# Building the M6 and M7 weight sums with accumulating transfers, and another order of the last products and scalings

## The chip, the cores and the metric

The kernel runs on one core of one Trainium2 chip. The metric is the device time in microseconds; the median of three runs before the change was 672.02 us (671.67 to 672.49). The core has a matrix engine (PE, with its weight loads shown as PEld), a vector engine (DVE), a scalar engine (ACT) and GpSimd (POOL). SyncE (SP) issues most transfers, and 16 DMA engines carry them out.

## The reference, cut to what matters

An encoder block: RMSNorm, one input projection, two attention mixers whose gated outputs are laid side by side, then an output projection, a residual sum and a last RMSNorm. The change lies wholly in the last part:

```python
mixed = jnp.concatenate([out_a, out_b], axis=-1)          # (512, 2048)
x = x + jnp.einsum('bsc,cd->bsd', mixed, w_out)           # 2048 x 2048
return rms_norm(x, final_norm_w)
```

## The kernel before, in words

All matrix products are made in three passes: each operand is split into a high part (rounded to float32r, the PE's format) and a low part (the rest), and high by high, high by low and low by high are summed (`three`, L1396). ACT makes high parts by copying, DVE or POOL makes low parts by subtracting.

The output has 512 tokens, four tiles of 128 rows (`t`), and 2048 columns in four blocks of 512 (`n`). Blocks 0 and 1 are made as plain products over `w_out`. Blocks 2 and 3 are made by Strassen's scheme with seven products M1 to M7 instead of eight: sums of the activations (`u_*`, or the parts of `mixed` as they are) times sums of weight pieces. This stage runs in 16 visits `v`. Each visit reads a buffer `t_raw[v % 4]` of four pieces of 512 columns (1 MB, slots 0 to 3) that SP loads from `w_pairs`. In visits 0 to 7, one sum is made (slots 2:4 become the difference). In visits 8 to 15:

- group 0 of the visit is slots 0:2: slot 0 becomes slot 0 + slot 1 (`part_sums`, L1257), the weights of M1; slot 1 is as loaded, for M5;
- group 1 is slots 2:4: they become slots 2:4 + slots 0:2 (L1255), the weights of M6 and M7.

For each group ACT makes the high part (`part_high`, L732), DVE the low part (`part_low`, L1264), and then PE runs its products: 12 matmuls for group 0 (M5, M1) and 12 for group 1 (M6, M7). DVE's order is fixed: low part of group 0 of visit v, the sums of visit v + 1, low part of group 1 of visit v. `t_hi` has two buffers and `t_raw` four, so ACT waits for PE to be done with the visit two before (`t_used`), and SP loads visit v when PE is done with visit v - 4. When visit 7 is through, DVE adds six finished PSUM banks into `y` (eight adds, `add`, L1277), and PE's products of visit 8 wait for them one after another (`y_added`), since they start in the same banks. In DVE's queue these eight adds stand behind the low part of group 1 of visit 8.

The last two visits, 14 and 15, run product by product: M1, M5, M6, M7 for the tiles 0 and 1 (`q` = 0), then the same for the tiles 2 and 3 (`q` = 1). Each is finished in turn (`m_done` 7 to 14); DVE adds it to `y`, and when a tile's blocks are complete ACT squares them (L705), DVE sums the squares (L1348), ACT takes the root (L790), DVE the reciprocal (L1352). Then each block of the tile is scaled: by ACT (L796), by POOL (L427), by DVE together with the gain `fw` (L1357), or alone (L1363), where POOL had multiplied the gain in ahead of time (`gained`, L402). The tiles come in the order 1, 0, 3, 2. SP stores a tile as two halves: the left one when `left[t]` is 2, the right one when `right[t]` is 2, strictly in this order (L325 to L329).

## Time and profile before

| | us |
|---|---|
| median of three runs | 672.02 |
| the profiled execution's own time | 671.85 |
| its span | 670.1 |
| PE busy | 654.7 (98%) |
| DVE busy | 442.2 (66%) |
| ACT busy | 331.3 (49%) |
| POOL busy | 280.1 (42%) |

The profiled execution is 0.17 us from the median, so its durations can be set against the runs. The span is what the profiler saw from first to last instruction; 1.75 us of the execution lie around it. PE is busy nearly all the time, so it sets the pace; the shares of the others are averages over stages, and say little of the last 60 us, where the change lies. A time there is given in us from the start of the span.

### The profile page before, as it was taken

To read this page: it belongs to the slowest core of one execution; us is meant where nothing else is said; L and a number is where in the kernel's file an instruction comes from. 1 tells how busy PE (TensorE), PEld (TensorE's weight loads), DVE (VectorE), ACT (ScalarE), POOL (GpSimd) and SP (SyncE) were. 2 spreads that over 40 slices of the span, in tenths; PEclk is the share of its full clock that TensorE was granted. 3 is DMA by queue.
4 is the path that set the end of the run, shared out by engine and by line. 5 is a ranking of instruction groups with operands and counts; after the bars stand their busy time and mean duration, and the time that the engine had idled before them with its cause. 6 is when DMAs were issued, how large, how long until landed. Compare 5 with 4: busy or idle time off the path is not lost. (4 is left out here: it accounts for less than half of the span.)

```text
span 670.1 us, 8800 instructions
## 1 busy us (share of the span) xinstructions
PE 654.7 (98%) x3126; PEld 548.4 (82%) x3126; DVE 442.2 (66%) x702; ACT 331.3 (49%) x623; POOL 280.1 (42%) x135
## 2 busy tenths in 40 slices
PE   9999999999999999999999999999999999999893
PEld 8888888888888888888888888888888888787782
DVE  6788132889684554654645667777553769899985
ACT  6743231311343753763664566877864533543534
POOL 0044443454244433433532526747868483020204
PEclk9999999999999999999999999999999999999997
DMA  8742322232232222222212413213124813576416
GB/s 293 256 141 96 103 94 95 83 105 95 94 94 96 75 83 95 92 65 95 95 64 94 126 35 124 64 64 96 32 72 177 299 65 113 233 259 236 180 64 251
DMA packets 21656, 81.96 MB, mean 122 GB/s; under 512 B 2416, under 2 KB 2672, under 8 KB 19568
## 3 DMA queue, kind: packets, MB, share of 16 engines
q1 hardware_dynamic: 18000, 73.41, 32.1%
q10 hardware_dynamic: 3616, 8.02, 3.4%
q8 instruction: 25, 0.41, 0.2%
q14 instruction: 15, 0.12, 0.1%
HBM read 77.22 MB, written 4.19 MB: 122 GB/s over the span
## 5 line engine op out<-in xcount | busy, mean ns | idle before, releaser
L337 POOL TENSOR_TENSOR w_lo<-w_raw,w_hi 128x1024 fp32r<-128x1024 f32 x84 | 206.0, 2458 | 269.7 <-ACT w_hi L442 269.6
L1398 PE MATMUL bank<-x_hi,w_hi 128*128 128x512 f32 x496 | 193.7, 390 | 0.0
L1401 PE MATMUL bank<-x_hi,w_lo 128*128 128x512 f32 x496 | 193.3, 390 | 0.0
L1402 PE MATMUL bank<-x_lo,w_hi 128*128 128x512 f32 x496 | 193.2, 390 | 0.0
L442 ACT ACTIVATE w_hi<-w_raw 128x1024 fp32r<-128x1024 f32 x93 | 98.1, 1055 | 130.0 <-PE bank L1398 109.1
L1402 PEld LDWEIGHTS bank<-x_lo,w_hi 128*128 128x128 f32 x496 | 93.1, 188 | 19.7
L1398 PEld LDWEIGHTS bank<-x_hi,w_hi 128*128 128x128 f32 x496 | 93.2, 188 | 18.8 <-DVE mixed L1078 0.5
L1401 PEld LDWEIGHTS bank<-x_hi,w_lo 128*128 128x128 f32 x496 | 93.2, 188 | 18.0
L402 POOL TENSOR_TENSOR y<-y,fw 128x512 f32<-128x512 f32 x11 | 17.6, 1616 | 80.1 <-ACT junk L705 44.4
L1398 PE MATMUL bank<-w_hi,mx_hi 128*128 128x512 f32 x128 | 50.3, 393 | 0.0
L1402 PE MATMUL bank<-w_lo,mx_hi 128*128 128x512 f32 x128 | 49.9, 390 | 0.0
L1401 PE MATMUL bank<-w_hi,mx_lo 128*128 128x512 f32 x128 | 49.9, 390 | 0.0
L732 ACT ACTIVATE t_hi<-t_raw 128x1024 fp32r<-128x1024 f32 (+1 forms) x32 | 29.8, 950 | 37.7 <-DVE t_raw L1257 19.5
L540 ACT ACTIVATE bank<-pa,st_a 128x128 f32<-128x128 f32 x64 | 22.8, 356 | 43.2 <-DVE st_a L992 43.2
L1264 DVE TENSOR_TENSOR t_lo<-t_raw,t_hi 128x1024 fp32r<-128x1024 f32 (+1 forms) x32 | 35.2, 1120 | 5.3 <-ACT t_hi L732 5.3
L1007 DVE TENSOR_TENSOR pta_lo<-bank,pta_hi 128x512 fp32r<-128x512 f32 x16 | 11.1, 692 | 32.1 <-ACT pta_hi L547 32.0
L1402 PEld LDWEIGHTS bank<-w_lo,mx_hi 128*128 128x128 f32 x128 | 24.0, 188 | 5.1
L1401 PEld LDWEIGHTS bank<-w_hi,mx_lo 128*128 128x128 f32 x128 | 24.1, 188 | 4.7
L895 DVE TENSOR_TENSOR t<-bank,sin_r 32x512 f32<-32x512 f32 x40 | 27.5, 687 | 0.5
L1398 PEld LDWEIGHTS bank<-w_hi,mx_hi 128*128 128x128 f32 x128 | 24.0, 188 | 4.6
L1015 DVE TENSOR_TENSOR mixed<-bank,o_low 64x256 f32<-64x256 f32 x32 | 13.5, 422 | 21.6 <-ACT o_low L554 21.4
L1398 PE MATMUL bank<-t_hi,mx_hi 128*128 128x512 f32 x64 | 25.3, 395 | 2.3 <-DVE t_lo L1264 2.2
(242 smaller groups left out, 1236.0 us busy)
## 6 DMA issues: line engine op xcount, KB each, us to landing
w_raw<-w_stream SPq DMA_DIRECT2D x93, 512.0 KB, 3.3
t_raw<-w_pairs SPq DMA_DIRECT2D x15, 1024.0 KB, 4.7
y<-x_nat ACTq DMA_DIRECT2D x4, 1024.0 KB, 5.3
out<-y SPq DMA_DIRECT2D x8, 512.0 KB, 3.0
xs<-x_t SPq DMA_DIRECT2D x4, 512.0 KB, 5.5
mixed<-x_t SPq DMA_DIRECT2D x4, 512.0 KB, 5.6
t_raw<-w_pairs ACTq DMA_DIRECT2D x1, 1024.0 KB, 7.7
fw<-final_w ACTq DMA_DIRECT2D x4, 256.0 KB, 5.6
```

The costliest lines, as they stand in the source:

```text
L337: pool.tensor_tensor(w_lo[:, s % HL, :], w_raw[:, s % RAW, :], w_hi[:, s % HL, :].bitcast(F32), ALU.subtract)\
L402: pool.tensor_tensor(y[:, t, cols], y[:, t, cols], fw[n][:, :], ALU.mult).then_inc(o_gained, 1)
L442: act.activation(w_hi[:, s % HL, :], w_raw[:, s % RAW, :], ACT.Copy).then_inc(w_hi_ready, 1)
L540: act.activation(B[4][:, P * k:P * k + P], pa[:, slot, k, :], ACT.Exp, bias=st[:, 1, k:k + 1], scale=A_SCALE, accum_out=st[:, 3, k:k + 1])
L732: act.activation(t_hi[v % 2][:, s, :], t_raw[v % 4][:, s, :], ACT.Copy).then_inc(t_high, 1)
L895: ins = dve.tensor_tensor(t2[32 * q:32 * q + 32, :], src[32 * o:32 * o + 32, :], sin[32 * q:32 * q + 32, :], ALU.mult)
L1007: dve.tensor_tensor(pta_lo[:, :], B[6][:, :], pta_hi[:, :].bitcast(F32), ALU.subtract).then_inc(a_pt_lo, 1)
L1015: ins = dve.tensor_tensor(out_e, by_head[h, e], o_low[h, :, :, :], ALU.add)
L1264: dve.tensor_tensor(t_lo[v % 4][:, s, :], t_raw[v % 4][:, s, :], t_hi[v % 2][:, s, :].bitcast(F32), ALU.subtract).then_inc(t_low[g], 1)
L1398: ins = pe.matmul(dst, ah, bh, start=start, stop=False, skip_group_check=goes_on)
L1401: pe.matmul(dst, al, bh, start=False, stop=False, skip_group_check=goes_on)
L1402: return pe.matmul(dst, ah, bl, start=False, stop=stop, skip_group_check=goes_on)
```

## The change

Three things are changed.

1. In visits 8 to 15 the group 1 sum is made by a transfer. When the load of visit v has landed, POOL issues a transfer that reads slots 0:2 from `w_pairs` in device memory once more (0.5 MB) and adds them to slots 2:4 in place. DVE's L1255 is gone; ACT's `part_high(v, 1)` waits for the new semaphore `t_added` instead. On POOL, the two gain products of block 2 now wait for DVE's low parts of visits 11 and 12.
2. In the last products for tiles 2 and 3, M6 comes ahead of M5. DVE's adds, ACT's squares and the row sums are put in an order that goes with it.
3. POOL scales with `tensor_tensor` and a broadcast operand instead of `tensor_scalar`, and takes over ACT's scaling of block 0 of tile 3.

```diff
+            def piece_added(v):
+                pool.wait_ge(t_landed[v % 4], 16 * (v // 4) + 16)
+                pool.dma_start(t_raw[v % 4][:, 2:4, :], w_pairs[v, :, 0:2, :], accum_op=ALU.add).then_inc(t_added[v % 4], 16)
+
             pool.wait_ge(fw1_landed, 16)
             for t in range(TOK):
                 pool.wait_ge(o_squared, 4 + t + 2)
                 pool.wait_ge(t_low[1], 4 + t)
                 gained(t, 1)
+                if t == 2:
+                    piece_added(8)
+            piece_added(9)
+            piece_added(10)
+            piece_added(11)
+            piece_added(12)
             pool.wait_ge(fws_landed, 32)
             for q in range(2):
                 pool.wait_ge(o_squared, 8 + q + 2)
+                pool.wait_ge(t_low[1], 12 + q)
                 gained(2 * q + 1, 2)
+                piece_added(13 + q)
+            piece_added(15)
...
-                pool.tensor_scalar(ys, ys, fin[:, t, 2:3], None, ALU.mult).then_inc(side[t], 1)
+                pool.tensor_tensor(ys, ys, fin[:, t, 2:3].to_broadcast([P, SEQ]), ALU.mult).then_inc(side[t], 1)
...
+            scale(2, 3, 0, 8, left)
             scale(2, 3, 1, 8, left)
...
                 if g == 0 and v < 8:
                     act.wait_ge(t_landed[v % 4], 16 * (v // 4) + 16)
+                elif g == 1 and v >= 8:
+                    act.wait_ge(t_added[v % 4], 16 * (v // 4) - 16)
                 else:
-                    act.wait_ge(t_summed, v + 1 if v < 8 else 2 * v - 6 - (g == 1))
+                    act.wait_ge(t_summed, v + 1)
...
             last_square(1, 3, 11, 13)
+            root(0, 1)
             last_square(0, 2, 12, 14)
-            root(0, 1)
+            root(1, 0)
             scale(0, 1, 2)
-            root(1, 0)
-            last_square(2, 3, 13, 17)
             scale(1, 0, 1)
-            last_square(3, 3, 14, 19)
+            last_square(3, 3, 13, 17)
+            last_square(2, 3, 14, 18)
+            root(2, 3)
             last_square(2, 2, 15, 20)
-            root(2, 3)
             root(3, 2)
-            scale(2, 3, 1)
             scale(3, 2, 2)
...
-                    dve.tensor_tensor(raw[:, 2:4, :], raw[:, 2:4, :], raw[:, 0:2, :], ALU.add).then_inc(t_summed, 1)
-                    dve.wait_ge(t_summed, 2 * v - 7)
                     dve.tensor_tensor(raw[:, 0, :], raw[:, 0, :], raw[:, 1, :], ALU.add).then_inc(t_summed, 1)
...
+            row_sum(0, 1, 13)
             add(0, 2, 0, 10, 12, op=ALU.subtract)
-            row_sum(0, 1, 13)
-            row_sum(1, 0, 14)
             reciprocal(0, 1)
             scale_gain(0, 1, 3)
+            row_sum(1, 0, 14)
             add(2, 2, 5, 11)
+            reciprocal(1, 0)
             add(3, 3, 5, 11, 4)
-            reciprocal(1, 0)
...
             m1(15, 1).then_inc(m_done, 1)
+            m6(14, 1)
+            m6(15, 1).then_inc(m_done, 1)
             m5(14, 1)
             m5(15, 1).then_inc(m_done, 1)
-            m6(14, 1)
-            m6(15, 1).then_inc(m_done, 1)
```

The rest of DVE's order at the end is shown below in its instructions. `add(3, 3, 7, ...)` stands for block 3 of tile 3 from bank 7.

POOL's queue from the gain products of block 1 to its end (`t_raw_60` to `t_raw_63` are the buffers 0 to 3), as the difference of the two:

```order
-L402 TENSOR_TENSOR y<-y,fw_169 128x512 [waits t_low1,o_squared] x3
-L402 TENSOR_TENSOR y<-y,fw_170 128x512 [waits o_squared,fws_landed]
-L402 TENSOR_TENSOR y<-y,fw_170 128x512 [waits o_squared]
+L402 TENSOR_TENSOR y<-y,fw_169 128x512 [waits t_low1,o_squared] x2
+L413 DMA t_raw_60<-w_pairs 128x1024 [waits t_landed0]
+L402 TENSOR_TENSOR y<-y,fw_169 128x512 [waits t_low1,o_squared]
+L413 DMA t_raw_61<-w_pairs 128x1024 [waits t_landed1]
+L413 DMA t_raw_62<-w_pairs 128x1024 [waits t_landed2]
```

The accumulating transfer of visit 8 stands ahead of the last gain product of block 1, those of 9 and 10 (and of 11 and 12) behind it.

DVE's queue around visit 8, before:

```order
L1255 TENSOR_TENSOR t_raw0_60<-t_raw0_60 128x1024 [waits t_landed0]
L1257 TENSOR_TENSOR t_raw0_60<-t_raw0_60 128x512 [waits t_summed]
L1264 TENSOR_TENSOR t_lo3_67<-t_raw3_63,t_hi1_69 128x1024 [waits t_high]
L1264 TENSOR_TENSOR t_lo0_64<-t_raw0_60,t_hi0_68 128x1024 [waits t_high]
L1255 TENSOR_TENSOR t_raw1_61<-t_raw1_61 128x1024 [waits t_landed1]
L1257 TENSOR_TENSOR t_raw1_61<-t_raw1_61 128x512 [waits t_summed]
L1264 TENSOR_TENSOR t_lo0_64<-t_raw0_60,t_hi0_68 128x1024 [waits t_high]
L1277 TENSOR_TENSOR y_147<-y_147,bank4 128x512 [waits m_done,y_landed]
```

and now:

```order
L1270 TENSOR_TENSOR t_raw0_60<-t_raw0_60 128x512 [waits t_landed0]
L1277 TENSOR_TENSOR t_lo3_67<-t_raw3_63,t_hi1_69 128x1024 [waits t_high]
L1277 TENSOR_TENSOR t_lo0_64<-t_raw0_60,t_hi0_68 128x1024 [waits t_high]
L1270 TENSOR_TENSOR t_raw1_61<-t_raw1_61 128x512 [waits t_landed1]
L1277 TENSOR_TENSOR t_lo0_64<-t_raw0_60,t_hi0_68 128x1024 [waits t_high]
L1290 TENSOR_TENSOR y_147<-y_147,bank4 128x512 [waits m_done,y_landed]
```

The two large sums are gone; the first of the eight adds still stands behind the low part of group 1 of visit 8 (the fifth row), whose high part now waits for the new transfer.

DVE's queue at the end of the tiles 3 and 2, from the first add of M1's bank 5, before:

```order
L1277 TENSOR_TENSOR y_147<-y_147,bank5 128x512 [waits m_done]
L1277 TENSOR_TENSOR y_147<-y_147,bank5 128x512 [waits y_added,m_done]
L1352 RECIPROCAL fin_83<-fin_83 128x1 [waits o_root]
L1277 TENSOR_TENSOR y_147<-y_147,bank3 128x512 [waits y_added,m_done] x2
L1277 TENSOR_TENSOR y_147<-y_147,bank7 128x512 [waits y_added,m_done]
L1357 SCALAR_TENSOR_TENSOR y_147<-y_147,fin_83,fw2_170 128x512 [waits o_recip]
L1277 TENSOR_TENSOR y_147<-y_147,bank1 128x512 [waits y_added,m_done]
L1348 TENSOR_REDUCE fin_83<-sumsq_82 128x1 [waits o_squared]
```

and now:

```order
L1290 TENSOR_TENSOR y_147<-y_147,bank5 128x512 [waits m_done]
L1365 RECIPROCAL fin_83<-fin_83 128x1 [waits o_root]
L1290 TENSOR_TENSOR y_147<-y_147,bank5 128x512 [waits y_added,m_done]
L1290 TENSOR_TENSOR y_147<-y_147,bank7 128x512 [waits y_added,m_done]
L1370 SCALAR_TENSOR_TENSOR y_147<-y_147,fin_83,fw2_170 128x512 [waits o_recip]
L1290 TENSOR_TENSOR y_147<-y_147,bank3 128x512 [waits y_added,m_done] x2
L1361 TENSOR_REDUCE fin_83<-sumsq_82 128x1 [waits o_squared]
L1290 TENSOR_TENSOR y_147<-y_147,bank1 128x512 [waits y_added,m_done]
```

The add of M6's bank 7, which completes tile 3, moves ahead of the two adds of M5's bank 3, and tile 3's sum of squares ahead of the last add.

## Rows read from the trace of the kernel before

**Rows 1.** The page: the whole span.
```profile
PE 654.7 (98%) x3126; PEld 548.4 (82%) x3126; DVE 442.2 (66%) x702; ACT 331.3 (49%) x623; POOL 280.1 (42%) x135
```
**Rows 2.** Busy time of each engine by stretch; then clock, DMA share, GB/s.
```profile
612.00:618.00 6.00, 5.65 (x23) 3.86 (x22) 6.00 (x10) 0.63 (x1) 0.00 (x0) 1.00 0.71 265
618.00:630.00 12.00, 10.05 (x44) 7.99 (x43) 10.80 (x9) 6.83 (x10) 3.53 (x2) 1.00 0.47 175
630.00:648.00 18.00, 18.00 (x81) 14.88 (x81) 15.91 (x16) 7.80 (x8) 0.00 (x0) 1.00 0.35 117
```
**Rows 3.** Timeline of PE's weight loads and matmuls: start, duration, instruction, idle before.
```profile
612.96 0.19 PEld L1398 LDWEIGHTS bank<-t_hi,u_hi 128*128 128x128 f32 x1 [0.55 <-DVE y L1277]
614.16 0.19 PEld L1398 LDWEIGHTS bank<-t_hi,u_hi 128*128 128x128 f32 x1 [0.66 <-DVE y L1277]
617.68 0.19 PEld L1398 LDWEIGHTS bank<-t_hi,u_hi 128*128 128x128 f32 x1 [0.26 <-DVE t_lo L1264]
628.09 0.19 PEld L1398 LDWEIGHTS bank<-t_hi,mx_hi 128*128 128x128 f32 x1 [2.37 <-DVE t_lo L1264]
...
657.74 0.39 PE L1401 MATMUL bank<-t_hi,mx_lo 128*128 128x512 f32 x1
657.97 0.39 PE L1402 MATMUL bank<-t_lo,mx_hi 128*128 128x512 f32 x1
```
**Rows 4.** Timeline of DVE, visits 8 to 12.
```profile
604.00 1.64 DVE L1255 TENSOR_TENSOR t_raw<-t_raw 128x1024 f32<-128x1024 f32 x1 [0.59 <-DMA t_raw<-w_pairs]
...
610.50 1.22 DVE L1264 TENSOR_TENSOR t_lo<-t_raw,t_hi 128x1024 fp32r<-128x1024 f32 x1
611.63 4.87 DVE L1277 TENSOR_TENSOR y<-y,bank 128x512 f32<-128x512 f32 x8
616.41 2.36 DVE L1264 TENSOR_TENSOR t_lo<-t_raw,t_hi 128x1024 fp32r<-128x1024 f32 x2
...
624.15 1.67 DVE L1257 TENSOR_TENSOR t_raw<-t_raw 128x512 f32<-128x512 f32 x1
625.74 3.43 DVE L1264 TENSOR_TENSOR t_lo<-t_raw,t_hi 128x1024 fp32r<-128x1024 f32 x2
...
630.34 0.69 DVE L1257 TENSOR_TENSOR t_raw<-t_raw 128x512 f32<-128x512 f32 x1
630.95 2.44 DVE L1264 TENSOR_TENSOR t_lo<-t_raw,t_hi 128x1024 fp32r<-128x1024 f32 x2
```
**Rows 5.** Groups by line from 540 us on: busy, mean ns, idle before.
```profile
L732 ACT ACTIVATE t_hi<-t_raw 128x1024 fp32r<-128x1024 f32 x24 | 25.0, 1058 | 33.8 <-DVE t_raw L1257 19.5 <-PE bank L1402 13.9 <-DVE t_raw L1253 0.4
L1255 DVE TENSOR_TENSOR t_raw<-t_raw 128x1024 f32<-128x1024 f32 x8 | 10.2, 1270 | 0.6 <-DMA t_raw<-w_pairs 0.6
```
**Rows 6.** DMA issues of the whole span: KB each, median us to landing.
```profile
t_raw<-w_pairs SPq DMA_DIRECT2D x15, 1024.0 KB, 4.7
out<-y SPq DMA_DIRECT2D x8, 512.0 KB, 3.0
t_raw<-w_pairs ACTq DMA_DIRECT2D x1, 1024.0 KB, 7.7
```
**Rows 7.** SP's queue, and bandwidth from 600 to 612 us in 40 slices.
```profile
603.34 0.33 SPq L324 DMA_DIRECT2D t_raw<-w_pairs  x1
GB/s 191 27 55 164 437 410 437 410 437 437 437 55 0 0 109 0 218 273 410 410 437 437 437 437 328 0 0 0 164 82 273 273 382 437 437 437 437 410 164 0
```
**Rows 8.** Timeline of the end: POOL, DVE, ACT and SP's queue.
```profile
652.47 1.30 POOL L402 TENSOR_TENSOR y<-y,fw 128x512 f32<-128x512 f32 x1 [25.52 <-ACT junk L705]
660.86 0.16 DVE L1352 RECIPROCAL fin<-fin 128x1 f32<-128x1 f32 x1 [0.91 <-ACT fin L790]
661.12 2.12 POOL L427 TENSOR_SCALAR y<-y,fin 128x512 f32<-128x512 f32 x1 [0.48 <-DVE fin L1352]
663.27 0.33 SPq L327 DMA_DIRECT2D out<-y  x1
```
**Rows 9.** Timeline of POOL: two gain products beside DVE's work.
```profile
623.42 3.53 POOL L402 TENSOR_TENSOR y<-y,fw 128x512 f32<-128x512 f32 x2 [18.87 <-ACT junk L705]
```

More of the change, by code:

```diff
@@ L266, in build @@
         fw1_landed = sem("fw1_landed")
-        t_landed = [sem(f"t_landed{n}") for n in range(4)]
+        t_landed, t_added = ([sem(f"{name}{n}") for n in range(4)] for name in ("t_landed", "t_added"))
         u_summed, u_high, u_low, p_summed, p_high, p_low = sem("u_summed"), sem("u_high"), sem("u_low"), sem("p_summed"), sem("p_high"), sem("p_low")
@@ L1370, in _ @@
             add(1, 3, 6, 9, 10)
+            row_sum(0, 1, 13)
             add(0, 2, 0, 10, 12, op=ALU.subtract)
-            row_sum(0, 1, 13)
-            row_sum(1, 0, 14)
             reciprocal(0, 1)
             scale_gain(0, 1, 3)
+            row_sum(1, 0, 14)
             add(2, 2, 5, 11)
+            reciprocal(1, 0)
             add(3, 3, 5, 11, 4)
-            reciprocal(1, 0)
-            add(2, 3, 3, 12, 6)
-            add(2, 2, 3, 12, 15, op=ALU.subtract)
-            add(3, 3, 7, 13, 16)
+            add(3, 3, 7, 12, 16)
             scale_gain(1, 0, 2)
-            add(2, 2, 1, 14, 18, op=ALU.subtract)
-            row_sum(2, 3, 16)
+            add(2, 3, 3, 13, 6)
+            add(2, 2, 3, 13, 15, op=ALU.subtract)
+            row_sum(2, 3, 15)
+            add(2, 2, 1, 14, 19, op=ALU.subtract)
             reciprocal(2, 3)
             scale_gain(2, 3, 3)
+            scale(2, 3, 2, 10)
             row_sum(3, 2, 17)
-            scale(2, 3, 2, 10)
             reciprocal(3, 2)
```

## The prediction

> **What bounds the kernel now.** I read the page first: PE is busy for 98% of the span [rows 1], so time is won only where PE stands still or where the end hangs behind its last product. The busy times by stretch then say where it stands still: in 630 to 648 not at all, in 612 to 618 for 0.35 us, in 618 to 630 for 1.95 us [rows 2]. The timeline of the weight loads names the places [rows 3]. A load runs one matmul ahead, so about 0.26 us of its idle time are made up: the idle of 0.55, 0.66, 0.26 and 2.37 us costs PE about 0.29, 0.40, 0 and 2.11 us, 2.80 in all. The first two wait for the eight adds behind visit 7, the long one for a low part of visit 10: all three for DVE. DVE's timeline shows why [rows 4]: from 604.0 on it works without a gap. Visit 8's large sum, the low part at 610.50 and then the eight adds, which start at 611.63, follow each other; the next low parts can't start ahead of 616.41; and around 624 to 629 its steps are stretched, the small sum to 1.67 us and two low parts to 3.43, where later visits show 0.69 and 2.44 [rows 4]. POOL runs two gain products there, 3.53 us [rows 9]. So of 2.80 us that can be won in this stretch, 2.11 depend on how much DVE has to do in visits 9 to 11, and 0.69 on when the eight adds start. The rest of the time until the last matmul at 657.97 [rows 3] PE paces itself.
>
> **Part 1, the sums by transfer: what goes.** Eight large sums of DVE, 10.2 us busy, 1.27 us each [rows 5], one in each visit. A visit has 24 matmuls at 0.23 us (the last two of [rows 3]), 5.4 us, and DVE then has two low parts (2.44) and a small sum (0.6 to 0.7) [rows 4] in it, 3.1 us. It has slack from there on. Does the 2.11 us stall at 628.09 go? Take the adds to start at 611.85 (below). They end at 616.65; two low parts of visit 9 take 2.3 (616.41 to 618.68 before), to 618.95; the small sum 0.6, to 619.6; ACT's copy 1.06 [rows 5], to 620.7; the low part 1.15, to 621.9; the next small sum, to 622.5; the low part that PE waited for, to 623.7. PE will want it after visits 8 and 9 and half of visit 10, at about 626. So 2.3 us are to spare and the stall goes: -2.11. The gain products that stretched DVE now wait for the low parts of visits 11 and 12 and fall later, at about 630 and 636; if they stretch DVE there by the 2.0 us seen before (1.67 - 0.69 and 3.43 - 2.44 [rows 4]), the 2.3 us of slack that each visit has covers it.
>
> **Part 1: what comes.** The high part of group 1 waits for load, then transfer, then ACT, then DVE. What is queued behind it matters: on DVE, behind the low part of group 1 of visit 8, stand the eight adds for which PE waits at once. Call L the time from visit 8's landing (604.0, when DVE's wait for it ends [rows 4]) to the landing of the accumulating transfer. POOL is free to issue it at once, since the gain product that held it is put behind it. Then the adds start at 604.0 + L + 1.06 (ACT's copy [rows 5]) + 1.13 (from 610.50 to 611.63 [rows 4]) + some 0.06 of semaphores = 606.25 + L. Before they started at 611.63, and PE lost 0.69 us. So visit 8 changes by (606.25 + L) - 611.63 = L - 5.4 us, and not below -0.69, which is reached at L = 4.7. With the -2.11 the whole stage changes by L - 7.5 us, at best by -2.8.
>
> No row shows an accumulating transfer, or one that POOL issues. From below, a plain store of as many bytes lands after 3.0 us; from above, the slowest load of twice the bytes after 7.7 us and two usual ones after each other after 9.4 (4.7 each) [rows 6]. Between the ends I build it from a load. Visit 9's load is issued at 603.34, its data flow from about 604.8 to 607.6 at up to 437 GB/s, the first 1.5 us after the issue [rows 7]. The new transfer's first data would come 1.5 us after 604.0, at 605.5, with 2.1 us of visit 9's data still to come on the same DMA engines. If only its 0.5 MB count (1.2 us at that rate), and the engines are shared evenly, it needs 2.4 us; if the read of its destination counts like another 0.5 MB, 2.4 us of its own and 2.1 of the other's, 4.5. With 0.6 us from last data to landing, as for visit 8's load (603.3 to about 604.0), L is 4.5 or 6.6. I take the middle, 5.6: the adds at 611.85, PE's stall in visit 8 0.9 instead of 0.7, the stage -1.9 us.
>
> The Trainium skill (DMA: Bandwidth & Descriptors, "Anatomy of one DMA — SWDGE (gpsimd) path") gives for a transfer issued by GpSimd some 2.0 us and its bytes over 436 GB/s, an estimate of 3.2 us for these 0.5 MB; it says nothing of accumulation, and no run here shows it yet. By that rule L would be under 4.7 and the stage -2.8.
>
> For visits 9 to 15 L costs nothing up to about 12 us: the load goes out when PE ends visit v - 4, and group 1 is wanted three and a half visits later, 19 us, of which 4.7 go to the load and 2.3 to ACT and DVE. 4 MB more cross the DMA engines in these 45 us, which were used to 0.71, 0.47 and 0.35 [rows 2]; SP's loads may land up to 1 us later, which the same 19 us cover. POOL's queue waits for nothing there that is late: visit 13's transfer stands behind a gain product that runs at about 630, when its load has just landed.
>
> **Parts 2 and 3, the end.** PE's number of matmuls is the same. With M6 ahead of M5, tile 3 is complete 1.36 us (six matmuls) earlier, and tile 2's block 3 as much later, where it isn't last: M7's product is. What ends the run is the stores. Of the last four, the first is issued at 663.27 when tile 3's left half is ready; and the end, 670.1, comes 6.8 us later: 2.1 MB at 437 GB/s are 4.8 us, and 1.5 from issue to first data and 0.6 behind the last [rows 7] make 6.9, so the last four stores run in a row. So the end moves with that first store, not with the last scaling. Before, tile 3's reciprocal came at 660.86 because ACT squared tile 2's last block ahead of its root; POOL then scaled one block in 2.12 us, to 663.24 [rows 8]. Now the root comes ahead of that square, and by ACT's and DVE's orders the reciprocal comes about 0.8 us earlier. But POOL does two blocks in a row. The new form, two operands, took 1.30 us for a gain product when DVE read one operand from its own memory [rows 8], and 1.77 when DVE's work had two (3.53 for two [rows 9]). Two blocks: 2.6, 3.5, or, if broadcasting costs what `tensor_scalar` did, 4.2 us. From about 660.2 that is 662.8, 663.7 or 664.4, against 663.24: -0.4, +0.5, +1.2. I take 1.6 each, nearest to the mixture beside it: +0.1.
>
> The Trainium skill (SBUF — State Buffer, "Who interferes with whom") says that a DVE instruction with two inputs in SBUF contends with GpSimd's reads. The trace agrees (1.30 against 1.77). DVE's scalings there have two such inputs, so by the rule alone the end would be +0.5; by the row without such a neighbour -0.4.
>
> **The sum.** -2.1 (stall in visit 10), +0.2 (visit 8), +0.1 (end) = -1.8 us. The profiled execution's own 671.85 becomes 670.05; from the median, 0.17 higher, 670.2.
>
> **The rivals.**
> - The transfer is short, L below 4.7. For it: the store's 3.0 us, and the row for 1 MB, 4.7. Against: it reads its destination too, and shares the engines. Stage -2.8, end +0.1: 669.3.
> - The saving is paid back in visit 8: L near 7.7, the slowest load of the trace. For it: every add waits behind this one transfer, and it comes just when visit 9's load has the engines full [rows 7]. Stage +0.2, end +0.1: 672.3.
> - Slower: an accumulating transfer is slow in itself. It decides from L = 8.8 on (8.8 - 7.5 = 1.3, the bound of what is told from no change). At L = 10, 2.5 us more: 674.6. For it: reading, adding and writing back may not be overlapped in the DMA engines as a copy is; two loads after each other are 9.4. Its place would be visit 8 alone, PE waiting for the adds for some 5 us.
> - That the transfers do the sums but DVE's relief is worth nothing, because the 2.11 us wait turns into one for ACT or POOL: the chain above has 2.3 us to spare, so little speaks for it. 671.9 or so.
>
> **How the numbers follow.** A measurement of this kernel tells about 0.2%, 1.34 us, from no change. The forecast holds 0.33, the short transfer 0.22, pay-back 0.25, slower 0.17, the last 0.03. The forecast's own range is L from 4.7 to 6.2, with the end's -0.4 to +0.5: 669.0 to 671.0. Faster, L below about 6.1: 0.55. Slower 0.18. Within: 0.27. The range: at the low end -2.8 and -0.4, 668.8; at the high end L = 9.4, +1.9, with the end's +0.1: 674.0.
>
> **What would show it.** In the new profile: the time from visit 8's landing to the start of ACT's copy of group 1 is L; DVE's eight adds start 2.2 us later; PE's only stall of note stands in visit 8, and none at visit 10; DVE has idle time in each of visits 10 to 15. At the end the store of tile 3's left half is issued 5.4 us after PE's last matmul starts, where it was 5.3. I would be wrong if L is above 6.2, if POOL issues the first transfer late, or if a wait for `t_added` shows up on PE's side in a visit other than 8.

## The result, and the profile after

The changed kernel takes **678.95 us** (median of 4 runs, 678.17 to 681.86); the kernel before, run beside it, 672.25 (671.67 to 673.46). The ratio is 1.0107, 95% interval 1.009 to 1.0124: slower by 6.7 us, where 670.2 was forecast, and outside the range (668.8 to 674.0). The profiled execution took 678.73 us by its own time, with a span of 676.9, against 671.85 and 670.1 before; both kernels are compared by these.

The page of the changed kernel answers to [rows 1] and [rows 6]:

```profile
PE 656.8 (97%) x3126; PEld 550.0 (81%) x3126; DVE 436.0 (64%) x694; ACT 330.7 (49%) x622; POOL 287.6 (42%) x144
...
t_raw<-w_pairs SPq DMA_DIRECT2D x15, 1024.0 KB, 5.7
...
t_raw<-w_pairs POOLq DMA_DIRECT2D x8, 512.0 KB, 7.6
out<-y SPq DMA_DIRECT2D x8, 512.0 KB, 3.5
```

DVE has eight instructions less, as forecast. The eight accumulating transfers take 7.6 us to land in the median for half a megabyte, longer than a load of a whole one took before (4.7), and the loads have become slower beside them.

The last matmul starts at 663.97, 6.0 us later than before [rows 3]; the span ends 12.9 us behind it, where it was 12.1. So 6.0 us arose while PE still multiplied and 0.8 at the end. The weight loads that waited longest name the places (start, duration, instruction, idle before it and what ended it):

```profile
615.66 0.19 PEld L1411 LDWEIGHTS bank<-t_hi,u_hi 128*128 128x128 f32 x1 [3.12 <-DVE y L1290]
616.86 0.21 PEld L1411 LDWEIGHTS bank<-t_hi,u_hi 128*128 128x128 f32 x1 [0.67 <-DVE y L1290]
...
647.12 0.19 PEld L1411 LDWEIGHTS bank<-t_hi,mx_hi 128*128 128x128 f32 x1 [0.91 <-DVE t_lo L1277]
...
652.87 0.19 PEld L1411 LDWEIGHTS bank<-t_hi,u_hi 128*128 128x128 f32 x1 [2.48 <-DVE t_lo L1277]
...
655.86 0.19 PEld L1411 LDWEIGHTS bank<-t_hi,mx_hi 128*128 128x128 f32 x1 [1.07 <-DVE t_lo L1277]
```

Less the 0.26 us that the load's lead makes up, these are 2.86 and 0.41 in visit 8, 0.65 in visit 13, and 2.22 and 0.81 for visit 15's two low parts: 6.95 us, against 2.80 before. The stall of visit 10 is gone. That leaves 1.8 of the 6.0 us, and they are in the clock. Busy time by short stretches behind visit 8's stall (PE, PEld, DVE, ACT, POOL, then granted clock, DMA share, GB/s):

```profile
616.00:618.00 2.00, 1.77 (x6) 1.15 (x5) 2.00 (x5) 0.00 (x0) 0.64 (x1) 0.74 1.03 344
618.00:620.00 2.00, 2.00 (x6) 1.54 (x6) 2.00 (x3) 1.06 (x1) 0.18 (x1) 0.50 1.04 256
620.00:622.00 2.00, 2.00 (x10) 1.61 (x9) 2.00 (x3) 0.00 (x0) 0.68 (x1) 0.90 1.03 218
622.00:624.00 2.00, 2.00 (x10) 1.68 (x9) 0.88 (x2) 1.90 (x2) 0.00 (x0) 1.00 1.00 276
```

From 616.9 to 620.4 the granted clock is 0.5, the lower level of 1.2 GHz (1.00 is 2.4 GHz); weight loads start 0.43 us apart instead of 0.23. Eight matmuls at 0.2 us more each: 1.7 us. So the 3.1 us of idle time (2.86 us of PE's) cost some 4.6. Before, no stretch of 612 to 648 was below 1.00 [rows 2], a stall of 2.37 us in it.

Visit 8's chain, which the prediction followed, in the timeline of POOL, ACT and DVE (it answers to [rows 4]; the transfer's issue is the row on POOL):

```profile
604.49 1.01 POOL L413 DMA_DIRECT2D t_raw<-w_pairs  x1 [3.64 <-DMA t_raw<-w_pairs]
```
```profile
612.10 2.00 ACT L748 ACTIVATE t_hi<-t_raw 128x1024 fp32r<-128x1024 f32 x2 [6.11 <-DMA t_raw<-w_pairs]
```
```profile
604.20 0.69 DVE L1270 TENSOR_TENSOR t_raw<-t_raw 128x512 f32<-128x512 f32 x1 [0.53 <-DMA t_raw<-w_pairs]
...
613.19 1.22 DVE L1277 TENSOR_TENSOR t_lo<-t_raw,t_hi 128x1024 fp32r<-128x1024 f32 x1 [3.46 <-ACT t_hi L748]
614.33 4.86 DVE L1290 TENSOR_TENSOR y<-y,bank 128x512 f32<-128x512 f32 x8
```

Visit 8 lands at 604.2 and its transfer at 612.1: L is 7.9 us, 5.6 was taken. The adds start 2.2 us behind it, as worked out, and PE loses 2.6 us more than before, where "L - 5.4" gives 2.5. The chain was right and L was not.

How full the DMA engines are, by the same stretches as [rows 2] and by queue from 600 to 660 us (packets, MB, share of all 16 engines):

```profile
612.00:618.00 6.00, 3.07 (x11) 1.91 (x10) 4.81 (x8) 2.00 (x2) 0.86 (x1) 0.91 1.04 333
618.00:630.00 12.00, 12.00 (x49) 9.79 (x49) 8.25 (x9) 7.30 (x11) 0.86 (x1) 0.90 0.99 268
630.00:648.00 18.00, 17.51 (x78) 14.20 (x77) 10.71 (x9) 5.77 (x6) 7.69 (x6) 1.00 0.95 250
```
```profile
q1 hardware_dynamic: 1152, 8.39, 38.5%
q0 software_dynamic: 1152, 4.19, 38.5%
...
t_raw<-w_pairs SPq DMA_DIRECT2D x7, 1024.0 KB, 7.9
t_raw<-w_pairs POOLq DMA_DIRECT2D x8, 512.0 KB, 7.6
```

Shares of 0.71, 0.47 and 0.35 [rows 2] became 1.04, 0.99 and 0.95, at a bandwidth far from the 437 GB/s seen in [rows 7]. The transfers' queue (q0) holds the engines as long as the loads' (q1) for half the bytes: 38.5% of 60 us over eight is 2.9 us of all 16 engines for each transfer. With 2.9 for each load that is 5.8 us of DMA for a visit of 5.4 us of matmuls.

The end, DVE's and POOL's timelines (they answer to [rows 8]):

```profile
667.39 0.15 DVE L1365 RECIPROCAL fin<-fin 128x1 f32<-128x1 f32 x1
```
```profile
667.63 2.48 POOL L440 TENSOR_TENSOR y<-y,fin 128x512 f32<-128x512 f32 x2 [2.69 <-DVE fin L1365]
```
```profile
670.14 0.33 SPq L327 DMA_DIRECT2D out<-y  x1
```

Tile 3's left half is stored 6.2 us after the last matmul (5.3 before, 5.4 forecast). POOL is not to blame: its two blocks take 1.24 us each, less than the 1.6 taken. The reciprocal comes 3.4 us after the last matmul, 2.9 before, where 0.8 less was forecast.

### The profile page after: what moved, and what is told of

The parts are those of the page before. It is cut to its first block, busy times and chain, and to the rows that moved or that the text cites. A ratio compares the mean times of both kernels' runs of the same rounds, so it can differ in the third digit from the quotient of the medians.

```text
span 676.9 us, 8799 instructions
## 1 busy us (share of the span) xinstructions
PE 656.8 (97%) x3126; PEld 550.0 (81%) x3126; DVE 436.0 (64%) x694; ACT 330.7 (49%) x622; POOL 287.6 (42%) x144
## 3 DMA queue, kind: packets, MB, share of 16 engines
q0 software_dynamic: 1152, 4.19, 3.4%
HBM read 81.42 MB, written 4.19 MB: 126 GB/s over the span
## 4 chain that ended last, share of the span: by engine, by line
PE 84%; DVE 7%; DMA 4%; issue 3%; ACT 2%; POOL 0%; DVEq 0%; ACTq 0%; POOLq 0%
PE bank L1411 25%; PE bank L1414 25%; PE bank L1415 25%; DMA t_raw<-w_pairs 4%; PE bank L1676 1%; DVE y L1290 1%; PE bank L1555 1%; PE bank L1565 1%; DVE p_sum L1257 1%; DVE t_raw L1268 1%; DVE t_lo L1277 1%; DVE u_lo L1246 1%; PE bank L1441 1%; PE bank L1662 1%; PE bank L1663 1%
## 5 line engine op out<-in xcount | busy, mean ns | idle before, releaser
L402 POOL TENSOR_TENSOR y<-y,fw 128x512 f32<-128x512 f32 x11 | 20.9, 1913 | 47.0 <-DVE t_lo L1277 35.7
```

Of the source, the lines that this page charges most:

```text
L402: pool.tensor_tensor(y[:, t, cols], y[:, t, cols], fw[n][:, :], ALU.mult).then_inc(o_gained, 1)
```

## The experiments

The expectations name their theories by letters. A: the addition makes a transfer take about twice the time of the DMA engines, so load and transfer fill them and pace the stage. B: the way through POOL makes a transfer late, whatever the load on the engines. C: visit 8's transfer is what costs. D: POOL's broadcast form slows DVE at the end. E: the stall of visit 10 came from POOL's gain products. F: the last visits have too little time between load and use.

**Part 1 and parts 2 and 3, apart.** `e1_part1` has the transfers and POOL's two waits with the end as before; `e2_parts23` the new end with DVE's large sums and neither transfers nor waits.

> Part 1 alone: the M6 and M7 sums by accumulating transfers and POOL's waits, with the end as before. The trace of the change shows the last matmul 6.0 us later (663.97 against 657.97) and 0.8 us more behind it (12.9 against 12.1). If that 0.8 belongs to parts 2 and 3, this kernel takes about 678.1 us (5.9 over before), the last matmul again near 664.0. If parts 2 and 3 interact with part 1, for example because DVE reaches the end in another state, it would differ from that by a microsecond or more either way.

> Parts 2 and 3 alone: DVE makes the sums as before, POOL's gain products don't wait for the low parts of visits 11 and 12; the order of the last products and the sharing of scalings as in the change. My prediction's step says the end moves by +0.1 (-0.4 to +1.2): 672.3 us. The trace of the change says +0.8 behind the last matmul: 673.0. With the last matmul at about 658.0 in either case; if it is later, the order of M6 and M5 costs PE something by itself.

Part 1 alone: 677.64 us (676.0 to 678.29), ratio 1.0061 (1.0037 to 1.0086). Its last matmul starts at 663.96, and its end is 12.5 us long: in this trace all of the loss before the end is its own (the profiled execution took 678.29 us, the longest of the four). Parts 2 and 3 alone: 673.26 (672.77 to 674.25), ratio 1.001 (0.9999 to 1.002), the end 13.05 us behind the last matmul at 658.55, 0.9 longer than before. What stretches it is on DVE. `e2_parts23`, timeline of DVE; before, each of these scalings took 0.75 us:

```profile
655.09 1.63 DVE L1380 SCALAR_TENSOR_TENSOR y<-y,fin,fw 128x512 f32<-128x512 f32 x1
...
658.75 1.38 DVE L1380 SCALAR_TENSOR_TENSOR y<-y,fin,fw 128x512 f32<-128x512 f32 x1
```

**POOL's form at the end.** `e5_scalar_pool` is `e2_parts23` with POOL's old instruction:

```
-pool.tensor_tensor(ys, ys, fin[:, t, 2:3].to_broadcast([P, SEQ]), ALU.mult)
+pool.tensor_scalar(ys, ys, fin[:, t, 2:3], None, ALU.mult)
```

> Parts 2 and 3 as in the run of parts 2 and 3 alone, but POOL scales with tensor_scalar as before, not with tensor_tensor and a broadcast operand. In that run DVE's two scalings with gain ahead of tile 3's row sum took 1.63 and 1.37 us where they took 0.75 before, beside POOL's new instructions. Theory D, the broadcast form takes DVE's second operand away: now DVE's two scalings take 0.75 again, tile 3's reciprocal comes 1.5 us earlier, POOL's two blocks take 4.2 instead of 2.5 us, and the store of tile 3's left half is issued at most 0.3 us sooner: 672.9 to 673.4 us, the loss merely moved. Rival, it is the new order of adds, squares and sums that is late: DVE's scalings stay long, or the reciprocal stays late, and the time goes up to 674.5 since POOL is slower.

672.78 us (672.1 to 673.89), ratio 1.0001 (0.999 to 1.0013). DVE's and POOL's timelines:

```profile
655.98 0.75 DVE L1380 SCALAR_TENSOR_TENSOR y<-y,fin,fw 128x512 f32<-128x512 f32 x1
...
658.78 0.74 DVE L1380 SCALAR_TENSOR_TENSOR y<-y,fin,fw 128x512 f32<-128x512 f32 x1
...
661.43 0.16 DVE L1375 RECIPROCAL fin<-fin 128x1 f32<-128x1 f32 x1
```
```profile
661.68 3.66 POOL L447 TENSOR_SCALAR y<-y,fin 128x512 f32<-128x512 f32 x2 [0.44 <-DVE fin L1375]
```

The last matmul starts at 659.45, so the reciprocal comes 1.98 us behind it: 0.9 earlier than before, which is the forecast's 0.8, and 1.5 earlier than in `e2_parts23`, as theory D had it. It is the broadcast form on POOL that stretches these scalings and took this away. But POOL then needs 3.66 us for its two blocks, and the store goes out 5.9 us behind the last matmul. Each form gives back what the new order wins. The two medians lie 0.5 us apart, with overlapping intervals.

The old form isn't free for DVE either. In `e1_part1` and seven more of the traces below that keep the old end (`e7` to `e11`, `e13`, `e14`) the second of DVE's scalings took 1.23 or 1.24 us beside `tensor_scalar` instead of 0.75, POOL's three blocks took 5.21 us instead of 5.75, and the end was 12.5 us long instead of 12.1:

```profile
664.53 1.24 DVE L1370 SCALAR_TENSOR_TENSOR y<-y,fin,fw 128x512 f32<-128x512 f32 x1
```

In `e6_pool_waits` and `e12_last_plain` it was 0.75 and 0.74 us, as before. No run shows what tips it one way or the other.

The trace of `e5_scalar_pool` (673.89 us, the longest of its ten executions) holds something else. It has the stall of visit 10 as the kernel before had it, 2.35 us against 2.37, but here the lower clock followed; weight loads, then busy times:

```profile
627.96 0.19 PEld L1421 LDWEIGHTS bank<-t_hi,mx_hi 128*128 128x128 f32 x1 [2.35 <-DVE t_lo L1287]
```
```profile
630.00:634.00 4.00, 4.00 (x14) 3.23 (x13) 3.97 (x5) 2.12 (x2) 0.00 (x0) 0.71 0.14 16
```

From 629 to 632 the granted clock was 0.50, and the last matmul of this execution came 1.5 us later than before.

**The addition left out.** `e3_plain_copy` is the changed kernel with `accum_op=ALU.add` struck from the transfer, so that M6's and M7's sums are not formed; the same bytes are written at the same place.

> The change with POOL's eight transfers as plain copies instead of accumulating ones: the same bytes from the same place over slots 2:4, so that the addition is left out. Theory A, accumulation is what costs: in the trace of the change a software transfer of 0.5 MB takes as much time on the 16 DMA engines as a load of 1 MB, so load and transfer together take 5.8 us of a visit's 5.4, and the engines pace the stage. A plain copy of 0.5 MB should take half of that, land in about 4.5 to 5.5 us, leave visit 8 a stall under 1 us and none later: 669.5 to 671 us. Rival B, it is the way through POOL (its issue, its descriptors) and not the addition: the time to landing stays at 7 us or more, visit 8's stall of 3 us and the slow clock behind it stay, 676 us or more.

671.72 us (670.91 to 677.45, 11 runs), ratio 0.9989 (0.9978 to 1.0): of 7.2 us between the two kernels all are due to the addition, by the medians. This is theory A's forecast (669.5 to 671) missed by 0.7 us, and far from B's (676 or more).

The profiled execution was the unusual one of 677.45 us. In its trace visit 8's load landed at 606.8, 2.6 us later than in the change, and PE had waited for low parts three times by then (0.37, 0.30 and 0.44 us, from 596 to 605), as it doesn't in the traces of the change and of `e15_plain_copy_again`. Its plain copy had L = 7.6 us, PE stood still for 3.72 us and the lower clock followed until about 624. So a plain copy can be as late as the accumulating one, here in one execution of eleven that was disturbed before. `e15_plain_copy_again` took the same kernel once more.

> The kernel with plain copies (the addition left out) once more, for a profile of a usual execution: the profiled one of the first run took 677.5 us against a median of 671.7. Expected 671.7, the copies landing after 4.5 to 6 us, visit 8's stall under 1.5 us with no slow clock, no stall over 0.6 us in visits 13 to 15.

671.38 us. ACT's timeline, and queues from 600 to 660 us:

```profile
610.00 2.01 ACT L748 ACTIVATE t_hi<-t_raw 128x1024 fp32r<-128x1024 f32 x2 [4.16 <-DMA t_raw<-w_pairs]
```
```profile
q1 hardware_dynamic: 1493, 9.65, 46.1%
q0 software_dynamic: 1152, 4.19, 20.5%
```

With a plain copy L is 5.8 us in this execution, almost the 5.6 that the forecast took, the copies land after 5.7 us in the median instead of 7.6, the same 4.19 MB hold the engines for 20.5% instead of 38.5%, and the clock is at 1.00 in every stretch. The last matmul starts at 656.67, 1.3 us before the old one. So this run is nearly what was forecast: 1.3 us won before the end (1.9 forecast; waits of 1.22 and 0.66 us stand in visit 8, and a new one of 0.49 near the end) and 0.8 lost at the end. The loads still take 7.3 us in the median, against 7.9 in the change and 4.8 before: late loads alone don't make PE wait.

**Adds ahead of the late low part.** `e4_adds_first` is the changed kernel with `part_low(8, 1)` behind the eight adds, which take PE's first two waits off the transfer.

> The change with one move in DVE's order: the eight adds of visit 8 ahead of the low part of its group 1, so that they no longer wait for the first transfer. Theory C, visit 8 is what costs: its 3.3 us stall behind the adds and the 1.7 us of matmuls at half clock behind it shrink to a stall of some 1.7 us for M6, and the kernel gains about 3.3 us, to 675.7. Theory A, the DMA engines pace the stage: what is gained in visit 8 is given back in visits 13 to 15, where PE waits for transfers by so much more, and the time stays within 1.3 us of the change's 679.

677.02 us (675.99 to 679.31), ratio 1.0072 (1.0044 to 1.01); 1.9 us less than the change by the medians, which the intervals don't separate (1.009 to 1.0124), and between the forecasts of C (3.3 less) and A (at most 1.3). The weight loads' waits in its trace (675.99 us, the shortest of four), and busy times behind the last of them:

```profile
615.23 0.19 PEld L1413 LDWEIGHTS bank<-t_hi,mx_hi 128*128 128x128 f32 x1 [1.71 <-DVE t_lo L1277]
629.48 0.19 PEld L1413 LDWEIGHTS bank<-t_hi,u_hi 128*128 128x128 f32 x1 [0.73 <-DVE t_lo L1277]
633.17 0.19 PEld L1413 LDWEIGHTS bank<-t_hi,mx_hi 128*128 128x128 f32 x1 [1.09 <-DVE t_lo L1277]
650.04 0.29 PEld L1413 LDWEIGHTS bank<-t_hi,u_hi 128*128 128x128 f32 x1 [2.68 <-DVE t_lo L1277]
```
```profile
650.00:652.00 2.00, 1.96 (x5) 1.59 (x6) 1.21 (x2) 0.76 (x1) 0.00 (x0) 0.50 0.00 0
```

Visit 8's stall shrinks from 3.3 to 1.45 us and the lower clock behind it goes, but 1.3 us of new stalls in visit 11 take part of that back, and now the lower clock follows visit 15's stall of 2.68 us, where it had stayed at 1.00 behind the change's 2.48. What was won in visit 8 is in large part paid later.

**POOL's waits alone.** `e6_pool_waits` is the kernel before with one line of the change:

```
                 pool.wait_ge(o_squared, 8 + q + 2)
+                pool.wait_ge(t_low[1], 12 + q)
                 gained(2 * q + 1, 2)
```

> The kernel before with one edit of the change alone: POOL's two gain products of block 2 wait for DVE's low parts of visits 11 and 12. Theory E, most of PE's 2.1 us stall in visit 10 comes from these products running beside DVE's sums (its steps are stretched by 2.0 us there): the stall at 628 shrinks to 0.1 to 0.3 us and the kernel takes 670.3 us. Rival, the products stretch DVE later instead and PE stalls as long in visit 12 or 13: 672.0 to 672.3.

670.92 us (670.62 to 672.25), ratio 0.9982 (0.9972 to 0.9992). PE's wait in visit 10 falls from 2.37 to 0.30 us, and a new one comes for visit 15:

```profile
626.05 0.19 PEld L1399 LDWEIGHTS bank<-t_hi,mx_hi 128*128 128x128 f32 x1 [0.30 <-DVE t_lo L1265]
646.95 0.19 PEld L1399 LDWEIGHTS bank<-t_hi,u_hi 128*128 128x128 f32 x1 [1.30 <-DVE t_lo L1265]
```
```profile
631.01 2.20 POOL L402 TENSOR_TENSOR y<-y,fw 128x512 f32<-128x512 f32 x1 [26.44 <-DVE t_lo L1265]
636.29 2.22 POOL L402 TENSOR_TENSOR y<-y,fw 128x512 f32<-128x512 f32 x1 [3.09 <-DVE t_lo L1265]
```

Theory E's stall of 0.1 to 0.3 us came true; its 670.3 us was missed by 0.6, for the new wait. About 1.4 us, most of the gain of 1.8 that was forecast for the whole change, comes from moving two gain products out of DVE's way, with no transfer at all.

**Transfers in some visits only.** All of these have part 1's form with DVE's large sum back in the other visits, and the end as before. `e7_two_visits` has transfers in visits 10 and 11 and no waits on POOL; the others have POOL's waits: visits 9 to 15, then 9, 11, 13, 15, then 9 alone, 9 to 13, and 9, 11, 13.

> The kernel before with accumulating transfers in visits 10 and 11 alone, without POOL's waits and with the end as before. Theory A (the DMA engines pace the stage when load and transfer come in every visit): with two transfers they have room, the stall of visit 8 stays 0.7, DVE saves 2.8 us ahead of the low part that PE waits for in visit 10, the 2.1 us stall goes, no stall comes in visits 13 to 15: 670.3 us. Rival B (a transfer through POOL is late whatever the load on the engines): it lands 7 to 8 us after the load also here.

> Part 1 for visits 9 to 15 only; visit 8's sum stays on DVE, the end as before. Theory C, visit 8's transfer is what costs (2.9 us of stall and 1.7 of half clock): 673 us or less, and no stall of note behind visit 8. Theory A, the engines pace the stage (5.8 us of load and transfer in a visit of 5.4): PE still waits 3 to 4 us in visits 12 to 15: 674 to 676 us.

> Part 1 for visits 9, 11, 13 and 15 only, with POOL's waits and the end as before. Theory A: load and transfer cost about 2.9 us each on all 16 DMA engines, so two visits now need 8.7 us of 10.9; the engines no longer pace the stage. Visit 9's sum goes from DVE's queue ahead of the eight adds, so these start 1.2 us earlier and visit 8's 0.7 us go; POOL's waits take the 2.1 us of visit 10; no stall in visits 13 to 15: 669.5 us. Rival B, the transfers are late whatever the load on the engines: they land 8 us or more after the load, and visits 13 and 15 still make PE wait: 671 us or more.

> The kernel before with one accumulating transfer, visit 9's, and POOL's waits. It is the version that the runs so far point to: the 0.7 us of visit 8 go since the adds start 1.2 us earlier, and the 2.1 us of visit 10 since POOL's gain products are out of the way (1.5 us were measured for the waits alone, which left a stall of 1.3 us in visit 14). 669.8 to 670.3 us. Rival: the transfer lands too late for visit 9's group 1 (wanted 10 us after its load), and a new stall stands there: 671 or more.

> Part 1 for visits 9 to 13 only, POOL's waits, the end as before. Visits 14 and 15 are multiplied product by product: PE wants visit 15's second group 2 visits and 12 matmuls (13.6 us) after visit 11's end, when its load is issued, not 19 us; with 4.7 us of load and 2.3 us of ACT and DVE that leaves 6.6 us for the transfer, which took 7 us and more in the change. Theory F, the short lead at the end is what costs behind visit 8: without transfers in 14 and 15 no stall over 0.5 us stands behind 640, and the time is 670.3 to 671. Theory A, crowded DMA engines (5.8 us of load and transfer in a visit of 5.4): the stalls of visits 10 to 13 (1.2, 0.4 and 0.3 us with transfers from visit 9 on) stay and PE waits 2 us more ahead of 647: 672.5 or more.

> Transfers in visits 9, 11 and 13 only, POOL's waits, the end as before: the run with every other visit, less visit 15. Theory F: its stall of 4.1 us in front of M6 of visits 14 and 15 goes, with the slow clock behind it; what is left is at most the 0.9 us in front of visit 10 that visit 9's late transfer costs, and DVE is relieved where its work is tight: 669.5 to 670.3 us, at or under the best so far (670.6). Rival: with a transfer in visit 13, DVE's low part of visit 14 is late all the same: over 671.

| transfers in visits | POOL's waits | median us (from, to) | ratio, 95% | last matmul |
|---|---|---|---|---|
| none | no | 672.3 | 1 | 657.97 |
| none (`e6`) | yes | 670.92 (670.62, 672.25) | 0.9982 (0.9972, 0.9992) | 657.08 |
| 9 (`e10`) | yes | 670.61 (670.03, 671.61) | 0.9973 (0.996, 0.9985) | 657.31 |
| 10, 11 (`e7`) | no | 670.95 (669.79, 671.95) | 0.9977 (0.9967, 0.9987) | 655.75 |
| 9, 11, 13 (`e14`) | yes | 670.63 (670.05, 674.19) | 0.9985 (0.9971, 0.9999) | 655.75 |
| 9 to 13 (`e13`) | yes | 672.33 (671.98, 673.17) | 1.0005 (0.9995, 1.0015) | 657.64 |
| 9, 11, 13, 15 (`e9`) | yes | 673.38 (671.17, 676.13) | 1.0014 (0.9996, 1.0032) | 660.39 |
| 9 to 15 (`e8`) | yes | 674.16 (672.47, 675.6) | 1.0028 (1.0015, 1.004) | 658.57 |
| 8 to 15 (`e1`) | yes | 677.64 (676.0, 678.29) | 1.0061 (1.0037, 1.0086) | 663.96 |

The last column is of the profiled execution, which lay up to 1.3 us from its median either way (`e8` 673.01 us, `e9` 674.68, `e10` 671.61).

By the medians, visit 8's transfer costs 3.5 us (677.64 - 674.16), those of 14 and 15 1.8 (674.16 - 672.33), and those of 9 to 13 1.4 (672.33 - 670.92), while every other one of these costs nothing (670.63). The differences are good to about 1 us, that of visit 8 to about 2, and 0.4 to 0.5 of the 1.4 is the longer end told above. That end also hides something: in `e7` and `e14` PE is through 1.3 us sooner than in `e6`, and the end is 0.5 longer.

Against the expectations: `e8` (674.16) is at the lower edge of A's 674 to 676, above C's 673. `e13` (672.33) lies nearer to A's 672.5 than to F's 671. `e9` (673.38) missed A's 669.5 by 3.9 and is on B's side, for visit 15's wait below. `e7` (670.95) missed its 670.3 by 0.6; `e10` and `e14` lie between forecast and rival. And B was right on one thing that A had otherwise: with few transfers they still landed late, after 9.7 us in the median in `e7` (two of them) and 7.9 in `e10` (one), each beside loads. Yet PE's waits behind them were short: 0.37 us in `e7`, 0.94 and 0.38 in `e10`.

Two traces show what the number of transfers does to PE's idle time. First `e13_visits_9_to_13`, then `e14_9_11_13`, from 618 us on:

```profile
618.00:630.00 12.00, 11.13 (x49) 8.56 (x48) 5.22 (x6) 6.56 (x10) 1.72 (x2) 1.00 1.03 313
```
```profile
618.00:630.00 12.00, 11.93 (x53) 9.54 (x52) 8.93 (x10) 8.05 (x12) 0.86 (x1) 1.00 0.87 259
```

At a DMA share of 1.03 PE is 0.87 us idle, at 0.87 it is 0.07. (In the change itself PE isn't idle in this stretch at 0.99; it is 4.6 us behind by then, so it wants everything later.) And `e9_every_other` shows that a visit's place counts beside its neighbours: visit 15's transfer, issued at 641.1, had the engines to 0.63 in 630 to 648 and still took 7.4 us. ACT's and PE's timelines:

```profile
648.52 1.06 ACT L755 ACTIVATE t_hi<-t_raw 128x1024 fp32r<-128x1024 f32 x1 [4.97 <-DMA t_raw<-w_pairs]
```
```profile
650.88 0.29 PEld L1422 LDWEIGHTS bank<-t_hi,mx_hi 128*128 128x128 f32 x1 [4.10 <-DVE t_lo L1288]
```

Its last 2 us moved at only 10 to 20 GB/s, which looks like a few DMA engines finishing late (no run here singled them out); and the clock was 0.86 in 648 to 660, the lower level again behind a long wait.

**The transfer by itself.** Visit 15's load is the last, so that nothing else is in flight while its transfer runs. `e11_last_alone` has the transfer in visit 15 only, `e12_last_plain` the same with the addition left out (M6's and M7's last sums are not formed). Each is one execution; the first took 672.3 us, the second 674.86. That second time isn't used: some 1.4 us arose before 615, ahead of any transfer, and the rest behind visit 10's stall, 2.35 us again, where the granted clock was 0.50 from 631 to 634.

> The kernel before with the accumulating transfer in visit 15 alone, whose load is the last one: nothing else is in flight. It measures the transfer by itself. Theory A (crowded DMA engines make it late): it lands after 4.5 to 5 us, against 6.1 to 9.8 in the change. Rival B (accumulating is slow by itself): after 7 us or more. The time stays within 1 us of before in either case.

> The same with a plain copy of the same bytes in place of the accumulating transfer (the addition in visit 15 is left out). If adding costs a second pass over the data on the DMA engines, the copy lands about 1.2 us (0.5 MB at 437 GB/s) earlier than the accumulating one, and its packets take half the time. If the way through POOL is the cost, both land alike.

The queues from 636 to 652 us, with the addition and then without:

```profile
q0 software_dynamic: 144, 0.52, 21.2%
q1 hardware_dynamic: 144, 1.05, 18.5%
...
t_raw<-w_pairs POOLq DMA_DIRECT2D x1, 512.0 KB, 5.6
```
```profile
q0 software_dynamic: 144, 0.52, 10.0%
...
t_raw<-w_pairs POOLq DMA_DIRECT2D x1, 512.0 KB, 4.4
```

Alone, the accumulating transfer takes 5.6 us to land and holds all 16 engines for 3.4 us (21.2% of 16), the plain copy 4.4 and 1.6: 2.1 times the engine time for the same bytes, and 1.2 us on the landing, as the expectation had it. The 5.6 us lie between A's forecast (4.5 to 5) and B's (7 or more). A load of twice the bytes holds them for 3.0 (18.5%).

## Why the prediction was wrong, step by step

Between the 670.2 us forecast and 678.95 lie 8.7 us: 2.3 for L, 3.7 for waits in visits 13 and 15 that had been put at nothing, 1.8 for the clock, 0.7 for the end and 0.2 for the median before, 672.25 instead of 672.02.

- **The 2.11 us stall of visit 10 goes: right in the time, not in the cause.** It is gone in the changed kernel, but in `e6_pool_waits` most of it goes without a transfer. The prediction knew that the gain products would be put later and counted that as harmless instead of as the remedy. `e7_two_visits` shows that relieving DVE by two sums does it as well; the two remedies do not add up.
- **"I take the middle, 5.6": the step that failed first.** L was 7.9 us, and visit 8 costs 2.5 us by the prediction's own formula with that number, where 0.2 was taken. The bounds were built for a transfer whose destination counts as as many bytes again. Alone, a transfer takes 5.6 us from issue to landing (`e11_last_alone`); beside visit 9's load and visit 9's own transfer, issued at 609.3, L is 7.9. The Trainium skill (DMA: Bandwidth & Descriptors, "Anatomy of one DMA — SWDGE (gpsimd) path") has 2.0 us and bytes over 436 GB/s, an estimate of 3.2; the trace disagrees, with 4.4 us for a plain copy alone and 5.6 for an accumulating one, and the text there speaks of no addition.
- **What no step had: the clock.** A stall of 3.1 us was followed by 3.5 us at the lower level, 1.7 us more (1.8 is what the sum of the waits leaves). The prediction's slower case priced its stall by its length alone: at L = 7.9 this adds more than half of what the stall itself adds.
- **"For visits 9 to 15 L costs nothing up to about 12 us": false, twice, and the dearest step, 3.7 us.** "Used to 0.71, 0.47 and 0.35" with 4 MB more were counted by bytes; by engine time each accumulated byte counts double, and 5.8 us of DMA per visit do not fit into 5.4, so the lead is used up. The loads went from 4.8 to 7.9 us in these 60 us; but with plain copies they took 7.3, so it is the transfers, 7.6 instead of 5.7, that the addition made late. That the doubled engine time is what makes them so is argued from the shares, and `e7` shows 9.7 us at a mean share of 0.88 (612 to 630). And 19 us of lead are not to be had at the end of the row, where visits 14 and 15 are multiplied product by product. Visit 15's group 1 is wanted (PE's queue waits for it ahead of M6 of visit 14) two visits and 12 matmuls after its load goes out, 13.6 us; load 7.9, transfer 7.3 and ACT and DVE 2.2 are 17.4. Its group 0 is needed three matmuls into visit 14, and ACT and DVE take it behind visit 14's group 1: from that load on there are three visits and three matmuls, 17.0 us, against 7.9 for the load, 0.9 behind a gain product on POOL, 7.5 for the transfer (641.8 to 649.4) and 3.5 for ACT and DVE, 19.8. The differences, 3.8 in all and 2.8, answer to the two waits seen, 2.48 and 1.07 us. An in-order engine hands the delay of one group to the next, which needed no transfer.
- **The end, +0.1: right in sign, mis-sized, +0.8 measured.** The reciprocal's 0.8 us came true with the old instruction of POOL (`e5_scalar_pool`); with the new one DVE's scalings went from 0.75 to 1.63 and 1.38 us. The prediction had the cause in hand and charged it to one side: POOL's blocks were given 1.6 us for the shared reads, and DVE's were left at their old duration. The rule of the Trainium skill (SBUF — State Buffer, "Who interferes with whom") names both sides, and these rows agree with it for the broadcast form (1.38 and 1.63 us); beside `tensor_scalar` the same scalings took 0.75 in most rows and 1.23 in others.
- **The rivals.** What came was the third, an accumulating transfer slow in itself, in its sign but not "in visit 8 alone". L, at 7.9, was that of the second rival, 7.7, which the prediction priced at 672.3; the rest is what no rival had, the clock and the waits of visits 13 and 15. So the threshold, L = 8.8, was too high. Of the theories of the experiments, A is the whole of the difference to a plain copy; the reckoning for visit 15 above is F's, and it needs A's late transfers to bite.

The sum of the differences between runs, from 672.3 us: POOL's waits -1.4, transfers of 9 to 13 +1.4, of 14 and 15 +1.8, of 8 +3.5, the end +0.9 (in the change itself +1.3 on top of part 1): 678.5, with 678.95 measured. The first four terms make up `e1_part1` by construction; what the sum tests is that part 1 and the end add up, and they do within 0.4 us.

Open stays why single accumulating transfers land after anything between 5.6 us (alone) and 11.0 us (`e1_part1`; 9.5 and 9.8 in `e7`, with only two). No version beats the line on POOL's wait for certain: 670.92 with it alone, 670.61 with visit 9's transfer and 670.63 with three are one and the same within their intervals, 1.4 to 1.7 us below the kernel before.

## What to carry to other kernels

A sum by an accumulating transfer is not paid in bytes but in time of the DMA engines, here twice that of a copy; add it to each stage's loads and compare with the stage's matmuls before trusting a mean share of the queues. Take one remedy at a time: a wait that was added to protect a change may be most of its gain. And when two engines slow each other, price it on both; and count with the slower clock that can follow a stall of PE, here 1.7 us behind one of 3.1.

## What the runs showed of the hardware

- An accumulating transfer of 0.5 MB from DRAM onto SBUF held 16 DMA engines for 3.4 us alone and 2.9 in a row of eight, a plain one for 1.6 and 1.5; its issue occupied POOL for 0.86 to 1.04 us, that of a plain copy for 0.53 to 0.74.
- The granted clock fell to 0.50 behind PE's stalls of 3.12 us (the change), 2.49 and 3.36 (`e1_part1`), 2.68 (`e4_adds_first`), 3.72 (`e3_plain_copy`), 4.10 (`e9_every_other`), and 2.35 (`e5_scalar_pool` and `e12_last_plain`). It stayed at 1.00 behind 2.37 (before), 2.36 (`e2_parts23`), 2.32 (`e11_last_alone`), 2.48 (the change, at 652.87) and 2.47 (`e8_from_visit_9`). The same stall of visit 10 stands on both lists, so its length alone doesn't tell.
- POOL's product with a broadcast operand took 1.02 to 1.24 us per 128x512 block where `tensor_scalar` took 1.7 to 2.1; beside the faster one DVE's scalings with two inputs took 1.38 and 1.63 us, beside the slower one 0.75 in most rows and 1.23 in others.
